# Two buffers for seven of a turn's twelve expert weight units, through the whole expert stage

## What is computed

```
def hier_moe(h, w_group, b_group, w_expert, b_expert, w_gate, w_up, w_down):
    """h: (N, D). Top-1 group, then top-2 experts within that group."""
    ...
    def expert(acc, prm):
        wg, wu, wd, gt = prm
        hid = jax.nn.silu(h @ wg) * (h @ wu)
        return acc + gt[:, None] * (hid @ wd), None

    out, _ = lax.scan(expert, jnp.zeros_like(h), (w_gate, w_up, w_down, gates.T))
    return out
```

## Time and profile before

| what | value |
|---|---|
| median of three executions | 664.0 us |
| profiled execution, its own time | 666.12 us |
| its span (first to last instruction) | 664.4 us |
| TensorE busy | 617.4 us (93%) |
| VectorE, ScalarE, GpSimd busy | 163.0, 131.6, 64.1 us |
| bytes moved, mean rate over the span | 249.22 MB, 375 GB/s |
| unit transfers, median from issue to landing (w_up, w_gate, w_down) | 23.6, 22.3, 19.4 us |

### The profile page before, as it was taken

The page is one execution under the profiler, slowest core; times in us unless marked ns, Lnnn a source line. Parts: engine busy times, 40 slices in busy tenths (PEclk is TensorE's granted clock), DMA queues, the critical chain, the costliest instruction groups (busy, mean ns, idle before and its releaser), DMA issues.

```text
span 664.4 us, 8875 instructions
## 1 busy us (share of the span) xinstructions
PE 617.4 (93%) x3449; PEld 321.6 (48%) x3451; DVE 163.0 (25%) x274; ACT 131.6 (20%) x289; POOL 64.1 (10%) x154
## 2 busy tenths in 40 slices
PE   5999999999979999999999999898989999898984
PEld 5886686544654353453543535253442535344431
DVE  3644577950851000100001000010100000010104
ACT  4111333450622111111111111111111111111112
POOL 4600030031002010110101101010110101000000
PEclk9899999999879999999999999999999999999998
DMA  8999999697558489999999999999999999999991
GB/s 311 324 346 387 411 407 386 248 422 322 221 221 362 178 311 425 421 421 423 421 423 422 421 423 420 424 420 420 424 419 425 419 424 420 422 421 421 422 382 67
DMA packets 44810, 249.22 MB, mean 375 GB/s; under 512 B 5265, under 2 KB 5325, under 8 KB 18157
## 3 DMA queue, kind: packets, MB, share of 16 engines
q1 hardware_dynamic: 42304, 244.33, 90.3%
q0 software_dynamic: 1008, 3.31, 1.4%
q10 hardware_dynamic: 1470, 1.22, 0.6%
HBM read 247.78 MB, written 1.07 MB: 375 GB/s over the span
## 4 chain that ended last, share of the span: by engine, by line
PE 47%; DMA 42%; DVE 6%; ACT 2%; issue 1%; SPq 1%; DVEq 0%; ACTq 0%
DMA W<-in_w_up_dram 38%; PE PS L1558 18%; PE PS L1573 5%; DMA W<-in_w_ada_dram 3%; PE PS L1231 3%; PE PS L1275 3%; PE PS L1489 3%; PE PS L1392 3%; PE PS L1287 2%; PE PS L1269 2%; PE PS L1531 1%; PE PS L1159 1%; PE PS L1588 1%; PE PS L1499 1%; DVE MOD L816 1%
## 5 line engine op out<-in xcount | busy, mean ns | idle before, releaser
L1558 PE MATMUL PS<-W,XT 128*64 128x512 f32 x1000 | 226.6, 595 | 20.4 <-DMA W<-in_w_up_dram 18.7
L1558 PEld LDWEIGHTS PS<-W,XT 128*64 128x64 f32 x1000 | 73.9, 137 | 155.8 <-issue 147.7
L1573 PE MATMUL PS<-W,HT 128*64 128x512 f32 x448 | 99.2, 595 | 0.0
L1102 DVE COPY XT<-PS 128x512 f32<-128x512 f32 x16 | 11.1, 691 | 249.1 <-PE PS L1489 249.1
L1573 PEld LDWEIGHTS PS<-W,HT 128*64 128x64 f32 x448 | 31.0, 137 | 60.9 <-issue 60.9
L1086 DVE SCALAR_TENSOR_TENSOR YL<-PS,gcol,YH 128x1024 fp32r<-128x1024 f32 x15 | 19.3, 1284 | 144.0 <-ACT YH L727 144.0
L1489 PEld LDWEIGHTS PS<-OH,H 128*128 128x128 bf16 x768 | 44.8, 115 | 12.2 <-issue 12.2
L1489 PE MATMUL PS<-OH,H 128*128 128x128 bf16 x768 | 47.1, 222 | 0.0
L816 DVE SCALAR_TENSOR_TENSOR MOD<-W,cS,MOD 128x2048 f32<-128x2048 f32 x16 | 37.6, 2348 | 11.2 <-DMA W<-in_w_ada_dram 10.7
L727 ACT ACTIVATE YH<-PS,gcol 128x1024 fp32r<-128x1024 f32 x15 | 16.7, 1113 | 97.9 <-PE PS L1573 97.9
L487 POOL COPY cur<-PG 128x4 f32 (+1 forms) x14 | 2.6, 186 | 299.5 <-PE PS L1521 299.3
(11 more groups left out here) (229 smaller groups left out, 520.6 us busy)
## 6 DMA issues: line engine op xcount, KB each, us to landing
W<-in_w_up_dram SPq DMA_DIRECT2D x64, 1024.0 KB, 23.6
W<-in_w_gate_dram SPq DMA_DIRECT2D x61, 1024.0 KB, 22.3
W<-in_w_down_dram SPq DMA_DIRECT2D x60, 1024.0 KB, 19.4
W<-in_w_ada_dram SPq DMA_DIRECT2D x16, 1024.0 KB, 7.9
W<-in_w_in_dram SPq DMA_DIRECT2D x12, 1024.0 KB, 7.6
W<-in_w_ada_dram SPq DMA_DIRECT2D x16, 512.0 KB, 5.5
W<-in_w_out_dram SPq DMA_DIRECT2D x4, 1024.0 KB, 7.4
V<-in_w_down_dram SPq DMA_DIRECT2D x4, 1024.0 KB, 14.5
```

Of the source, the lines that this page charges most:

```text
L1558: last = nc.tensor.matmul(PS[rows, u // 2, :], XT[:, k, rows], unit_at(i, odd, unit_of(u, which), p)[:, q * FF:(q + 1) * FF], start=(k == ...
L1573: last = nc.tensor.matmul(PS[rows, 2 + q % 2, :], HT[:, k, rows], unit_at(i, odd, unit_of(u, which), p)[:, q * FF:(q + 1) * FF], start=(k ...
```

## The change

The diff gives units 8 to 11 (`EVEN_OWN`) and 0 to 2 (`ODD_OWN`) two homes each for the whole of the first pass. In even turns units 8 to 11 lie in V0 to V3, and units 0 to 2 in W; in odd turns units 8 to 11 lie in W, and units 0 to 2 in V4, V5 and Hn. Units 3 to 7 keep their one buffer in W. The waits for arrival go by a semaphore for each of the seven extra buffers.

The issue of the first 19 units is as it was. The rest is done by `refill(turn, units)`: for each unit number in order it waits until that unit of turn `turn - 1` is used, and fetches into the buffer that has just come free. For the seven units with two homes that is the unit of turn `turn + 1`; for units 3 to 7 it is that of turn `turn`. The loop over turns is written out instead of being a hardware loop. The further passes (`more_pass`) use W alone, as before.

```
--- before.py
+++ after.py
@@ -34,8 +34,9 @@
 TURNS = N_EXPERTS // 2
 LAST_TWO = TURNS // 2 - 1
 ONEHOTS = 2 * TT + 1
-SPARES = (8, 9, 10, 11)
-AHEAD_SPARES = (0, 1, 2)
+EVEN_OWN = (8, 9, 10, 11)
+ODD_OWN = (0, 1, 2)
+TWO_HOMES = ODD_OWN + EVEN_OWN
 
 
 def prologue_units():
@@ -158,7 +159,7 @@
         diag = MOD[:, D:2 * D].rearrange("p (n q) -> p n q", n=N_DIFF * TT)
 
 
-        V = [sb(f"V{n}", [P, UW]) for n in range(len(SPARES) + 1)]
+        V = [sb(f"V{n}", [P, UW]) for n in range(len(EVEN_OWN) + 1)]
         H3 = sb("H3", [P, 3, TT, D], bf16)
         XT = sb("XT", [P, DC, 2 * SLOTS])
         SG = sb("SG", [P, FC, 2 * SLOTS])
@@ -180,7 +181,7 @@
 
 
         unit_in = [sem(f"unit_in{s}") for s in range(RING)]
-        spare_in = {u: sem(f"spare_in{u}") for u in SPARES + AHEAD_SPARES}
+        own_in = {v: sem(f"own_in{v}") for v in TWO_HOMES}
         ada_used, first_used, win_used = sem("ada_used"), sem("first_used"), sem("win_used")
         first_in = {n: sem(f"first_in{n}") for n, unit in enumerate(UNITS) if unit[0] == "first"}
         bank_zero = sem("bank_zero")
@@ -286,22 +287,27 @@
 
             return 2 * u + which
 
-        def is_spare(i, odd, v, p):
-
-            return p == 0 and isinstance(i, int) and i == 0 and v in (AHEAD_SPARES if odd else SPARES)
-
-        def unit_at(i, odd, v, p):
-
-            return V[(SPARES + AHEAD_SPARES).index(v)] if is_spare(i, odd, v, p) else W[slot_of(BASE + v)]
+        def in_own(odd, v, p):
+
+            return p == 0 and v in (ODD_OWN if odd else EVEN_OWN)
+
+        def home(odd, v, p):
+
+            return V[(EVEN_OWN + ODD_OWN).index(v)] if in_own(odd, v, p) else W[slot_of(BASE + v)]
+
+        def landing(odd, v, p):
+
+            return own_in[v] if in_own(odd, v, p) else unit_in[slot_of(BASE + v)]
 
         def unit_arrived(eng, i, odd, v, p):
 
-            if is_spare(i, odd, v, p):
-                eng.wait_ge(spare_in[v], 16)
-                return
-            first = isinstance(i, int) and i == 0 and odd == 0 and p == 0
-            fills = uses_of(BASE + v) + odd + TURNS * p - (v in SPARES or (v in AHEAD_SPARES and not first))
-            eng.wait_ge(unit_in[slot_of(BASE + v)], i * 32 + 16 * fills)
+            if in_own(odd, v, p):
+                eng.wait_ge(own_in[v], i * 16 + 16)
+            elif p == 0 and v in TWO_HOMES:
+                eng.wait_ge(unit_in[slot_of(BASE + v)], i * 16 + 16 * uses_of(BASE + v))
+            else:
+                fills = uses_of(BASE + v) + odd + TURNS * p - (TURNS // 2 if v in TWO_HOMES else 0)
+                eng.wait_ge(unit_in[slot_of(BASE + v)], i * 32 + 16 * fills)
 
         def both_used(eng, units):
 
@@ -357,54 +363,58 @@
                 else:
                     load(n, w_out[0].rearrange("(h k p) n -> h p k n", h=4, p=P)[a])
 
-            def fetch(v, e, into, landed):
-                sp.dma_start(into[:], unit_source(e, v // 2)).then_inc(landed, 16)
-
-            def stream(p):
+            def fetch(v, odd, e, p=0):
+                sp.dma_start(home(odd, v, p)[:], unit_source(e, v // 2)).then_inc(landing(odd, v, p), 16)
+
+            def ready_at_first(v, odd):
+
+                if not in_own(odd, v, 0):
+                    wait_reader(BASE + v - RING)
+                elif not odd:
+                    sp.wait_ge(pt_mm, PAIRS)
+                    if v > EVEN_OWN[1]:
+                        sp.wait_ge(pv_mm, PAIRS)
+                        sp.wait_ge(gained, 2)
+                elif v == ODD_OWN[0]:
+                    sp.wait_ge(gained, 2)
+                elif v == ODD_OWN[1]:
+                    sp.wait_ge(h_ready, 2 + TT)
+                else:
+                    sp.wait_ge(h3_ready, TT)
+
+            def refill(turn, units):
+
+                for v in units:
+                    into = turn + 1 if v in TWO_HOMES else turn
+                    sp.wait_ge(unit_used[v % 2], UPE * (turn - 1) + v // 2 + 1)
+                    fetch(v, into % 2, 2 * into + v % 2)
+
+            def first_pass():
+                for v in range(UPT):
+                    ready_at_first(v, 0)
+                    fetch(v, 0, v % 2)
+                for v in EVEN_OWN + ODD_OWN:
+                    ready_at_first(v, 1)
+                    fetch(v, 1, 2 + v % 2)
+                last = TURNS - 1
+                for turn in range(1, last - 1):
+                    refill(turn, range(UPT))
+                refill(last - 1, [v for v in range(UPT) if v not in EVEN_OWN])
+                refill(last, [v for v in range(UPT) if v not in TWO_HOMES])
+                refill(last - 1, EVEN_OWN)
+
+            def more_pass(p):
                 first = TURNS * UPE * p
                 for v in range(UPT):
-                    if p == 0 and v in SPARES:
-                        sp.wait_ge(pt_mm, PAIRS)
-                        if v > SPARES[1]:
-                            sp.wait_ge(pv_mm, PAIRS)
-                            sp.wait_ge(gained, 2)
-                        fetch(v, v % 2, V[SPARES.index(v)], spare_in[v])
-                        continue
-                    if p == 0:
-                        wait_reader(BASE + v - RING)
-                    else:
-                        sp.wait_ge(unit_used[v % 2], first - UPE + v // 2 + 1)
-                    fetch(v, v % 2, W[slot_of(BASE + v)], unit_in[slot_of(BASE + v)])
-                if p == 0:
-                    for v in SPARES:
-                        wait_reader(BASE + v - RING)
-                        fetch(v, 2 + v % 2, W[slot_of(BASE + v)], unit_in[slot_of(BASE + v)])
-                    for v in AHEAD_SPARES:
-                        if v == 0:
-                            sp.wait_ge(gained, 2)
-                        elif v == 1:
-                            sp.wait_ge(h_ready, 2 + TT)
-                        else:
-                            sp.wait_ge(h3_ready, TT)
-                        fetch(v, 2 + v % 2, V[len(SPARES) + v], spare_in[v])
-                    for v in AHEAD_SPARES:
-                        sp.wait_ge(unit_used[v % 2], v // 2 + 1)
-                        fetch(v, 4 + v % 2, W[slot_of(BASE + v)], unit_in[slot_of(BASE + v)])
-                    for v in range(UPT):
-                        if v not in SPARES + AHEAD_SPARES:
-                            sp.wait_ge(unit_used[v % 2], v // 2 + 1)
-                            fetch(v, 2 + v % 2, W[slot_of(BASE + v)], unit_in[slot_of(BASE + v)])
-                    for v in range(UPT):
-                        if v not in AHEAD_SPARES:
-                            sp.wait_ge(unit_used[v % 2], UPE + v // 2 + 1)
-                            fetch(v, 4 + v % 2, W[slot_of(BASE + v)], unit_in[slot_of(BASE + v)])
-                with sp.Fori(3 if p == 0 else 1, TURNS) as i:
+                    sp.wait_ge(unit_used[v % 2], first - UPE + v // 2 + 1)
+                    fetch(v, 0, v % 2, p)
+                with sp.Fori(1, TURNS) as i:
                     for v in range(UPT):
                         sp.wait_ge(unit_used[v % 2], i * UPE + (first + v // 2 + 1 - UPE))
-                        fetch(v, i * 2 + v % 2, W[slot_of(BASE + v)], unit_in[slot_of(BASE + v)])
-
-            stream(0)
-            more_passes(sp, most_tokens(sp), stream)
+                        fetch(v, 0, i * 2 + v % 2, p)
+
+            first_pass()
+            more_passes(sp, most_tokens(sp), more_pass)
             out_v = out[0].rearrange("(t p) d -> p t d", p=P)
             for part in range(2 * TT):
                 t, cols = part // 2, slice(part % 2 * 512, part % 2 * 512 + 512)
@@ -1556,7 +1566,7 @@
                             for which in (0, 1):
                                 rows = halves_of(which)
                                 last = nc.tensor.matmul(PS[rows, u // 2, :], XT[:, k, rows],
-                                                        unit_at(i, odd, unit_of(u, which), p)[:, q * FF:(q + 1) * FF],
+                                                        home(odd, unit_of(u, which), p)[:, q * FF:(q + 1) * FF],
                                                         start=(k == 0), stop=(k == DC - 1))
                                 if q == 3:
                                     last.then_inc(unit_used[which], 1)
...
```

More of the change, by code:

```diff
@@ L1588, in last_down @@
                                 last = nc.tensor.matmul(PS[rows, 2 + q % 2, :], HT[:, k, rows],
-                                                        unit_at(LAST_TWO, 1, unit_of(u, which), p)[:, q * FF:(q + 1) * FF],
+                                                        home(1, unit_of(u, which), p)[:, q * FF:(q + 1) * FF],
                                                         start=(k == 0), stop=(k == FC - 1))
```

## The result

Ten executions of the changed kernel gave a median of 665.45 us, ten of the kernel before, on the same chip, 663.91 us. The ratio is 1.0025 with a 95% interval of 1.0014 to 1.0036, so 0.9 to 2.4 us more. Forecast were 665.0 us and +1.1 us. The profiled execution has a span of 665.2 us.

The account below looks back on a forecast made before the run. TensorE was taken as late until about 254 us, transfers as the bound from turn 6. 7 x 2.487 - 13.9 + 0.3 + 27.09 - 29.79 = +1.1 us on 664.0 gave 665.0 us, range 662.9 to 667.6.

Parts of the forecast that it names:

- The hole, 13.9 us: Transfers ran at 249 instead of 422 GB/s from 220 to 254 us; closing this is worth 13.9 us.
- the loss of 0.3 us for a rate of 413 with few units outstanding: In the closed hole, two or three units outstanding run at 413 GB/s over some 12 us, losing 0.3 us.
- Seven units ahead, 17.4 us: The new issue order puts seven more units ahead of each turn's unit 7, 2.487 us each, 17.4 us.
- t.7 lands 3.8 us later: Unit 7 of every turn that waits for it lands 3.8 us later: 17.4 us minus 13.6 us of head start.
- Waiting starts in turn 5: TensorE's waits for transfers begin in turn 5 instead of 6; the size of a turn's wait doesn't change.
- the 2.7 named as a sign: Sign in the profile after: TensorE waits for w_gate and w_up about 2.7 us a turn in turns 5 to 14.
- TensorE is the bound in the last turn: From the last pair of turn 14 to that of turn 15 TensorE needs 27.09 us, where before it took 29.79.
- The rest is nothing: SyncE's written-out loop, TensorE's instructions and buffer parity, the first 19 issues and the granted clock were taken as costing nothing.
- the first (all of the transfer time comes back): Rival: all 13.9 us of transfer time comes back, 650.1 us, needing the queue's order to cost nothing; 10%.
- The second: Rival: more than 13.9 us is recovered, with 2.4 us of apparent landing lag also coming from the hole, 662.6 us; 14%.
- third: Rival: the stream fed unit by unit doesn't get up to rate from 220 to 246 us, losing 6 us, 671 us; 20%.
- the fourth: Rival: SyncE, stopping at each wait in order, never gets ahead, so the change has no effect, 664.0 us; 6%.

Follow-up runs that it names:

- switch experiments: Five kernels: changed kernel's buffers, first 19 issues and fetch order up to unit 7 of a chosen turn, then TensorE's order of use; 651.08 to 660.99 us.
- run with the cut end: Changed kernel, but only 16 of 2048 columns transferred for the nine last units (15.3 to 15.11): 665.96 us, ratio to before 1.0021.
- loop written out: Kernel before with its own buffers and order, only SyncE's loop over turns 3 to 15 written out: 664.25 us, ratio 1.0011.
- end cut: Kernel before, SyncE's loop written out, only 16 of 2048 columns transferred for turn 15's twelve units: 661.53 us, ratio 0.9957.
- the switch at 6 and 7: Changed kernel, its fetch order kept up to unit 6.7 or 7.7, then TensorE's order of use: 651.74 us and 651.08 us.
- the switches at 3 and 11: Changed kernel, its fetch order kept up to unit 3.7 or 11.7, then TensorE's order of use: 655.88 us and 657.62 us.

## Why the prediction was right

- *The hole, 13.9 us, closes.* It did: 420 GB/s in its place. Of the loss of 0.3 us for a rate of 413 with few units outstanding little is seen; 236 to 244 us ran at 419.
- *Seven units ahead, 17.4 us.* The switch experiments show it: with the same closed hole, taking these seven from in front of the later units is worth 14.0 us (665.45 to 651.4, the mean of the two best), where the sum gave 15 (665.0 to 650). By the length of the stage it is 12.8 us against the profile of the changed kernel, and 14.2 against its run with the cut end, which restarted as slowly as these two.
- *t.7 lands 3.8 us later.* 14.7 came 4.0 us later by the clock. Counted from the start of `down` in turn 0 it was 3.2 us (395.9 against 392.7), and 4.6 us in the run with the cut end, whose stream is the same up to there. The forecast lies between. Most of the 1.4 us can be read at the restart (changed kernel, then its run with the cut end):

```profile
196.49:220.49 24.00, 23.14 (x167) 11.00 (x166) 5.17 (x19) 3.52 (x10) 6.15 (x19) 1.00 0.79 322
```

```profile
193.99:217.99 24.00, 23.15 (x167) 11.03 (x166) 5.15 (x19) 3.52 (x10) 6.13 (x19) 1.00 0.77 305
```

  That is 24 x 17 / 421 = 1.0 us of stream. In the kernel before such a loss doesn't reach the end: with 303 GB/s at the restart (loop written out) and with 322 (end cut) 14.7 came 392.4 and 392.6 us after the start of `down` of turn 0, and the bytes missing at the restart (24 x 19 = 456 KB) moved in the hole: in the next 20 us the former ran at 217 GB/s and the latter at 195, 20 x 22 = 440 KB. The changed kernel has no hole left to absorb it. The sum has no term for this.
- *Waiting starts in turn 5.* Yes: 0.64 us ahead of 5.7, at 343.73 us. The idle time comes to 20.7 us in turns 5 to 14, 2.1 a turn, and not to the 2.7 named as a sign; it is the distance from one t.7 to the next, 29.85 us against TensorE's 27.09, that shows 2.8.
- *TensorE is the bound in the last turn.* Shown twice: 27.1 us with the stream complete early, and no change when its last 22 us are taken away.
- *The rest is nothing.* The written-out loop is nothing that can be measured, and the granted clock stayed at 1.00.

The sum was 0.4 us short of the measured +1.5 us, and inside the interval. The mechanism was right in each step above; that the size fits to 0.4 us is in part luck, since the length of the stage grew by 0.5 us in one profile of this stream and by 1.9 in the other. Of the rivals the first (all of the transfer time comes back) failed on the condition that it named: the order of the queue does cost. With that cost removed, its 650.1 us is within 1.6 us of what was measured. By the length of the stage 12.2 and 12.4 of its 13.9 us came back. The second and third fell with the landing of 14.7 and the rate of 420 GB/s from 220 us on, the fourth with the issues at 220.14.

## What to carry to other kernels

A second buffer makes a fetch possible earlier, but in a queue that is already full each early fetch stands in front of one that is wanted sooner. So count, for each unit that the consumer waits for, the bytes issued ahead of it: refill early while the stream would otherwise idle, and go back to the order of use while the consumer still has enough turns to profit. A gain in a stream that is banked until the end is worth only as much as the consumer can catch up in the turns that are left.

## What the runs showed of the hardware

Once the stream ran, its rate hardly depended on how many units of 1 MiB were outstanding: 416 to 418 GB/s from 220 to 230 us in the profile of the changed kernel, where about one and a half to four were (my estimate from the issues and the bytes moved), 419 at 236 to 244 us, 420 to 422 later. A unit issued into an empty queue moved 262 GB/s over its four microseconds.

A start into an empty queue can cost more than its first unit. In the run with the cut end the engines moved 320 GB/s at 202 to 206 us, though about three units were outstanding (the same estimate). In the same place, from 12 to 8 us before the start of `down` of turn 0, the runs with the switch at 6 and 7 and the one with the loop written out had the same dip, 297 to 334 GB/s, and the kernel before a slight one, 393. The changed kernel, the switches at 3 and 11 and the kernel before with its end cut had none, 418 to 426. What makes the dip stays open.
